# Diffusion block in f32 on one core: delta rule inverse in 32x32 blocks, attention heads in pairs, norm sums in few rows

## The reference

```
q, k = l2norm(q), l2norm(k)
# delta rule, in chunks: g is the cumulated gate
a   = strict_lower((k * beta) @ k.T * decay)
sol = triangular_solve(a + I, [v * beta, k * beta * exp(g)])
u, w = sol
v_new = u - w @ S
o     = (q * exp(g)) @ S + ((q @ k.T) * decay) @ v_new
S     = S * exp(g_last) + (k * exp(g_last - g)).T @ v_new
# both attentions
p = softmax(q @ k.T * scale [+ bias]);  o = p @ v
```

## Time and profile before

| what | us |
|---|---|
| median of 3 runs | 3280.55 (3277.18 to 3281.9) |
| the profiled execution | 3280.95 |
| its span in the trace | 3279.1 |
| TensorE busy | 2745.0 (84%), 13516 passes |
| VectorE busy | 1122.5 (34%) |
| ScalarE busy | 526.0 (16%) |
| GpSimd busy | 380.5 (12%) |

### The profile page before, as it was taken

The page is one execution under the profiler, slowest core; times in us unless marked ns, Lnnn a source line. Parts: engine busy times, 40 slices in busy tenths (PEclk is TensorE's granted clock), DMA queues, the critical chain, the costliest instruction groups (busy, mean ns, idle before and its releaser), DMA issues. The chain is left out here.

```text
span 3279.1 us, 34031 instructions
## 1 busy us (share of the span) xinstructions
PE 2745.0 (84%) x13516; PEld 1506.2 (46%) x13516; DVE 1122.5 (34%) x2055; ACT 526.0 (16%) x984; POOL 380.5 (12%) x380
## 2 busy tenths in 40 slices
PE   5899996778887679999999878999846685889896
PEld 3345563778776522222222236655736572222221
DVE  0143422454543512222222331740077733212123
ACT  1222116222221200000000010320222211000000
POOL 0000000444430000000000000000035400000000
PEclk9889997899998889999999879999968897999998
DMA  6300115100004268788887701101100134999996
GB/s 245 132 26 20 40 40 185 45 1 1 1 1 148 77 225 291 292 304 293 301 292 292 258 26 64 33 23 50 63 0 1 54 140 168 409 410 410 410 409 255
DMA packets 161760, 527.46 MB, mean 161 GB/s; under 512 B 13808, under 2 KB 49008, under 8 KB 155120
## 3 DMA queue, kind: packets, MB, share of 16 engines
q1 hardware_dynamic: 149920, 492.93, 40.1%
q10 hardware_dynamic: 7632, 18.27, 1.5%
q0 software_dynamic: 4096, 14.68, 1.4%
HBM read 516.93 MB, written 8.91 MB: 160 GB/s over the span
## 5 line engine op out<-in xcount | busy, mean ns | idle before, releaser
L1113 PE MATMUL bank<-arena 128*128 128x128 f32 x2208 | 271.2, 283 | 21.4 <-DVE arena L1285 19.7
L1113 PEld LDWEIGHTS bank<-arena 128*128 128x128 f32 x2208 | 263.6, 198 | 27.9 <-issue 24.5
L2037 PE MATMUL bank<-ring,arena 128*64 128x512 f32 x1024 | 258.9, 614 | 7.7 <-ACT arena L2092 7.2
L1993 PE MATMUL bank<-ring,arena 128*64 128x512 f32 x1024 | 245.6, 600 | 22.9 <-DMA ring<-in_moe_w_up_dram 22.8
L2128 DVE TENSOR_TENSOR arena<-arena,bank 128x512 f32<-128x512 f32 x160 | 109.9, 687 | 440.7 <-PE bank L1965 440.5
L1978 PE MATMUL bank<-ring,arena 128*64 128x512 f32 x1024 | 249.9, 609 | 10.6 <-DMA ring<-in_moe_w_gate_dram 9.4
L445 PE MATMUL bank<-arena,ring 128*128 128x384 f32 (+1 forms) x704 | 244.1, 509 | 2.7 <-ACTq L2288 1.5
L1965 PE MATMUL bank<-arena 128*128 128x512 f32 (+1 forms) x320 | 193.2, 687 | 44.8 <-DVE arena L2128 39.7
L445 PEld LDWEIGHTS bank<-arena,ring 128*128 128x128 f32 x704 | 134.4, 191 | 111.0 <-issue 33.0
L475 PE MATMUL bank<-ring,arena 128*128 128x256 f32 (+1 forms) x800 | 170.4, 375 | 6.9 <-ACTq L2288 6.9
L436 DVE COPY arena<-bank 128x384 f32<-128x384 f32 (+4 forms) x60 | 30.3, 505 | 423.2 <-PE bank L445 230.9
(11 more groups left out here) (304 smaller groups left out, 3411.3 us busy)
## 6 DMA issues: line engine op xcount, KB each, us to landing
ring<-in_moe_w_gate_dram SPq DMA_DIRECT2D x128, 1024.0 KB, 6.7
ring<-in_moe_w_up_dram SPq DMA_DIRECT2D x128, 1024.0 KB, 7.9
ring<-in_moe_w_down_dram SPq DMA_DIRECT2D x128, 1024.0 KB, 8.3
ring<-in_w_mod_dram SPq DMA_DIRECT2D x48, 1024.0 KB, 5.1
ring<-in_odd_w_in_dram SPq DMA_DIRECT2D x16, 1024.0 KB, 5.5
ring<-in_even_w_in_dram SPq DMA_DIRECT2D x10, 1024.0 KB, 10.3
ring<-in_even_w_out_dram SPq DMA_DIRECT2D x4, 1024.0 KB, 11.5
tok_lat_dram<-X ACTq DMA_DIRECT2D x8, 512.0 KB, 2.7
```

The costliest lines, as they stand in the source:

```text
L1113: mm = nc.tensor.matmul(heads(out[:, :])[:, h, :], lhs(h), rhs(h), start=start, stop=stop)
L1993: mm = nc.tensor.matmul(U_[half(hf), :], xl[:, k, :], columns(u, kk, hf), start=k == 0, stop=k == KB - 1)
L2037: mm = nc.tensor.matmul(D_[half(hf), :], HT[:, f % 4, half(f // 4)], columns(c, kk, hf), start=f == 0, stop=f == KB - 1)
```

## The change

It does five things.

- Delta scan: the inverse is built in 32x32 blocks. The four diagonal blocks of the four heads lie side by side in one 128x128 tile (`ATC`, `TTC`, `TC`, `WC`). Level 0 is a mask and a subtraction on VectorE, and a 32x32 block transpose there instead of the one on TensorE. Levels 1 to 4 multiply blocks only: 16 block products, a copy by ScalarE, 16 block products, a subtraction and a block transpose by VectorE. GpSimd spreads the blocks on the diagonal of the full inverse. Level 5 joins pairs of blocks, level 6 the two halves of 64, both writing into it. The two full products with the decay are made by VectorE between the levels. GpSimd makes the last right side (`KL`) at its end, with a wait of its own on TensorE.
- Both attentions: the unit is a pair of heads. 64-row products of the two heads alternate, in the neighbourhood attention their 64-column value products too. Score banks 0 to 3 belong to one pair at a time, turned tiles have banks 4 to 6, outputs bank 7. In the neighbourhood attention ScalarE scales the context scores (`plain`), and four bias tables are held instead of two.
- Norm: sums of four blocks go to four groups of 32 partitions, all eight into two banks; one logarithm and one exponential serve all; TensorE spreads the rows again, and VectorE multiplies out of PSUM in half blocks.
- Constants: 784 more columns (masks of 32x32 blocks, the block diagonal, selection rows and columns).
- The second scan uses twelve of the first scan's semaphores and adds 12 to each number it waits for. Its instructions stay.

The diff, cut to its core (removed code is left out for the most part, and so are changes that only rename):

```diff
...
+            parts[f"small{d}_{l}"] = np.concatenate([parts[f"level{d}_{l}"][b:b + 32, b:b + 32] for b in range(0, P, 32)])
+    parts["diag32"] = r // 32 == c // 32
...
+    parts["one_col"] = np.concatenate([np.broadcast_to(c[:, 0:32] == j, (P, 32)) for j in range(2)], 1)
+    parts["one_row"] = np.concatenate([np.broadcast_to(r % 32 == j, (P, P)) for j in range(2)], 1)
...
+                def front(p):
+                    parts, _ = segments(p)
+                    if p:
+                        nc.tensor.wait_ge(at_neg if biased(p) else at_exp, b + 2 * p)
+                    if pairs[p]["main"]:
+                        for e in range(2):
+                            for n, a, keys in parts:
+                                pairs[p]["main"](score(e, n)[:, 0:keys], e, n)
+                    for n, a, keys in parts:
+                        for e in range(2):
+                            mm = pairs[p]["tail"](score(e, n)[:, 0:keys], e, n)
+                            if n == len(parts) - 1:
+                                mm.then_inc(at_s, 1)
...
+                def values(p):
+                    tiles = segments(p)[1] // P
+                    nc.tensor.wait_ge(at_pt, bp + p + 1)
+                    if p:
+                        nc.tensor.wait_ge(at_oc, bp + p)
+                    if pairs[p]["together"]:
+                        for j in range(tiles):
+                            for e in range(2):
+                                mm = nc.tensor.matmul(out_rows(p, e), pairs[p]["v"](j, e), pt[:, tiles * e + j, :],
...
+                for p in range(np_ + 1):
+                    if p + 1 < np_:
+                        front(p + 1)
+                    if p:
+                        values(p - 1)
+                    if p < np_:
+                        turn(p)
...
+                for p in range(np_ + 1):
+                    if p < np_:
+                        if biased(p):
+                            plain(p)
+                        exps(p)
+                    if p:
+                        turned(p - 1)
...
+                            nc.vector.wait_ge(*loaded_)
+                            dv.then(nc.vector.scalar_tensor_tensor(r[:, 0:keys], score(e, n)[:, 0:keys], scale, bias,
+                                                                   ALU.mult, ALU.add))
+                            nc.vector.wait_ge(at_raw, i + 1)
+                            dv.then(nc.vector.tensor_reduce(m[:, 0:1], r[:, 0:total], AX.X, ALU.max))
...
+                mod.pe_rows(range(4))
+                for j in range(2):
+                    nc.tensor.wait_ge(nm_sq, 4 * j + 4)
+                    for bk, a, b_ in sums:
...
+                            mm = nc.tensor.matmul(bk[32 * g:32 * (g + 1), 0:b_ - a], one_col[:, j, :], SQ[g][:, a:b_],
+                                                  start=j == 0, stop=j == 1)
                     mm.then_inc(nm_sum, 1)
...
+                nc.tensor.wait_ge(nm_rs, 1)
+                for u, (i, hf) in enumerate(units):
+                    rows = slice(32 * (i % 4), 32 * (i % 4 + 1))
+                    if u >= len(spread):
+                        nc.tensor.wait_ge(nm_out, u - len(spread) + 1)
+                    nc.tensor.matmul(spread[u % len(spread)][:, 0:HALF], one_row[rows, i // 4, :], RS[rows, hf * HALF:(hf + 1) * HALF],
+                                     start=True, stop=True).then_inc(nm_bc, 1)
+                mod.pe_rows(range(4, KB))
...
+                    for l in range(1, 5):
+                        for d in range(2):
+                            nc.tensor.wait_ge(gd["bt"], step(n, l - 1, d, 4))
+                            nc.tensor.wait_ge(gd["tc"], step(n, l - 1, d, NS))
+                            for h in range(H):
+                                for i in range(NB):
+                                    mm = nc.tensor.matmul(compact(d, 2)[blk(i), h, :], BT[d][l][blk(i), h, :], TC[d][blk(i), h, :],
+                                                          start=True, stop=True)
+                            mm.then_inc(gd["u"], 1)
+                        for d in range(2):
+                            nc.tensor.wait_ge(gd["ucopy"], step(n, l - 1, d, NW))
+                            for h in range(H):
+                                for i in range(NB):
+                                    mm = nc.tensor.matmul(compact(d, 0)[blk(i), h, :], WC[d][blk(i), h, :], TTC[d][blk(i), h, :],
+                                                          start=True, stop=True)
+                            mm.then_inc(gd["upd"], 1)
...
+                            for s_, t_ in pairs32(d):
+                                mm = nc.tensor.matmul(compact(d, 2)[blk(t_), h, :], AT[d][blk(s_), h, blk(t_)], TC[d][blk(s_), h, :],
+                                                      start=True, stop=True)
...
+                            mm = nc.tensor.matmul(half64(d, 2)[far, h, :], AT[d][near, h, far], T64[d][near, h, :], start=True, stop=True)
+                        mm.then_inc(gd["u"], 1)
...
+                            mm = nc.tensor.matmul(half64(d, 0)[near, h, :], W64[d][far, h, :], TT[d][far, h, far], start=True, stop=True)
+                        mm.then_inc(gd["upd"], 1)
...
+                            nc.scalar.activation(WC[d], compact(d, 2), ACT.Copy).then_inc(gd["ucopy"], 1)
...
+                            nc.gpsimd.tensor_tensor(BT[d][l], ATC[d], small_mask(d, l), ALU.mult).then_inc(gd["bt"], 1)
+                    for d in range(2):
+                        nc.gpsimd.wait_ge(gd["tc"], step(n, 4, d, NS))
+                        nc.gpsimd.tensor_tensor(in_blocks(TT[d], NB), over_blocks(TTC[d], NB), diagonal(slice(0, P), range(NB)),
+                                                ALU.mult).then_inc(gd["asm"], 1)
...
+                        nc.gpsimd.wait_ge(gd["qkd"], 2 * n + d + 1)
...
+                        nc.gpsimd.wait_ge(gd["u"], step(n, 5, d, NW))
+                        nc.gpsimd.tensor_tensor(KL[d], heads(KTOK[:, tl, :]), gcol(EL, d, tl), ALU.mult).then_inc(gd["kl"], 1)
...
+                        for i in range(NB):
+                            nc.vector.tensor_tensor(ATC[d][blk(i), :, :], heads(bk(d, 3)[:, :])[blk(i), :, blk(i)], ETM[d][blk(i), :, blk(i)],
+                                                    ALU.mult).then_inc(gd["atc"], 1)
+                        nc.vector.wait_ge(gd["atc"], NB * (g + 1))
+                        dv.then(nc.vector.tensor_tensor(TTC[d], ATC[d], small_mask(d, 0), ALU.mult))
+                        dv.then(nc.vector.tensor_tensor(TTC[d], ident32, TTC[d], ALU.subtract))
+                        nc.vector.transpose(TC[d].rearrange("p h c -> p (h c)"), TTC[d].rearrange("p h c -> p (h c)")).then_inc(gd["tc"], 1)
+                    for l in range(1, 5):
+                        for d in range(2):
+                            nc.vector.wait_ge(gd["upd"], step(n, l - 1, d, NW))
+                            dv.then(nc.vector.tensor_tensor(TTC[d], TTC[d], compact(d, 0), ALU.subtract))
+                            nc.vector.transpose(TC[d].rearrange("p h c -> p (h c)"),
+                                                TTC[d].rearrange("p h c -> p (h c)")).then_inc(gd["tc"], 1)
+                            if l == 4:
+                                near = halves64(d)[0]
+                                nc.vector.wait_ge(gd["tc"], step(n, 4, d, NS))
+                                dv(nc.vector.tensor_tensor(in_blocks(T64[d][near, :, :], 2), over_blocks(TC[d][near, :, :], 2),
+                                                           diagonal(near, range(2 * d, 2 * d + 2)), ALU.mult))
+                        if l < 3:
+                            attention_of(n, l - 1)
+                        else:
+                            queries_of(n, l - 3)
...
+                        nc.vector.tensor_scalar(T64[d][blk(t_), :, SB * (s_ - 2 * d):SB * (s_ - 2 * d + 1)], compact(d, 2)[blk(t_), :, :], -1.0, None,
+                                                ALU.mult).then_inc(gd["t5"], 1)
+                        for s_, t_ in pairs32(d):
+                            nc.vector.tensor_scalar(TT[d][blk(s_), :, blk(t_)], compact(d, 0)[blk(s_), :, :], -1.0, None,
+                                                    ALU.mult).then_inc(gd["t5"], 1)
+                    for d in range(2):
+                        near, far = halves64(d)
+                        nc.vector.wait_ge(gd["upd"], step(n, 5, d, NW))
+                        nc.vector.tensor_scalar(TT[d][near, :, far], half64(d, 0)[near, :, :], -1.0, None, ALU.mult).then_inc(gd["tfin"], 1)
...
+        HG_STEP = dict(sig="in", cr="kbt", qk="diff", att="exps", att_used="pair", fin="qe", qfin="attn", turn="qkd", turncopy="rhs",
+                       out="kl", done="sol", zero="ws")
+        hg, HG_0 = {x: gd[y] for x, y in HG_STEP.items()}, 2 * NT
...
+                                    nc.tensor.wait_ge(hg["sig"], HG_0 + 2 * n + d + 1)
...
```

554 lines of the change are left out of this document (288 added, 266 removed).

## The result

The changed kernel takes 3109.5 us (median of 4 runs, 3101.4 to 3112.4) against 3280.3 of before on the same chip: ratio 0.948, 95% interval 0.946 to 0.950. That is 170.8 us less, where 152 were forecast, and the time lies in the forecast's own range. The profiled execution has a span of 3110.5 us.

A forecast was written before the change was run, and what follows sets the result against it. It took waits between engines to bound the scan, ScalarE to be nearly always busy in the norm, TensorE to bound both attentions. Gains of 105 + 18 + 10 + 20 - 1 = 152 us gave 3129, own range 3085 to 3175.

The forecast's parts named there:

- Levels 1 to 4: Scan step: block levels of 3.0 us each, 12 us for four, with 0.8 us per group of 32 passes.
- The way in: Scan step before the levels: seven instructions, 2.1 us per direction, 4.2 for both; 2.25 us gained a step.
- Levels 5 and 6: Scan step: joining blocks into the full inverse, 3.5 us for level 5 and 4.1 for level 6.
- The low clock: Scan step: small blocks leave the array mostly idle, the clock ends low, and the solution products lose 2.0 us.
- the 0.8 for GpSimd: Scan step: GpSimd's block diagonals and four products finish after levels 5 and 6, delaying the solution: 0.8 us lost.
- The second rival: Scan inverse: instruction supply holds TensorE at 0.112 us a pass, total 3431 us; chance 0.12, of which 0.10 slower.
- break-even of 0.072: Scan inverse: from 0.072 us a pass on, the changed kernel turns slower than before.
- The first rival: Scan block products: four row groups write one PSUM bank and go in file, 1.25 us a group, total 3179; chance 0.17.
- The half blocks: Norm: VectorE multiplies 16 half blocks of 384 columns out of PSUM, 0.56 us each, 9.0 us together.
- the wait behind the scores, 4.8: Latent attention, per pair: two maxima, one exponential and hand-overs take 4.8 us after 4.3 us of scores.
- The third rival: Both attentions: pairing heads gains nothing, as the single-buffered chain needs 1.4 us more per pair; total 3159, chance 0.11.
- the sign that the prediction set, under 70%: Neighbourhood attention: pairs 6.8 us apart with TensorE under 70% busy would show the forecast.

The follow-up runs named there:

- e5: Changed kernel with half the block products in levels 1 to 4, each twice as wide, the second head's inverse left out: 3092.6 us.
- e2: Changed kernel with the block product loops of levels 1 to 4 swapped, four heads of one diagonal block in a row: 3125.1 us.
- e6: Changed kernel with 32 more recorded TensorE passes of 128x128, results unread, before the levels of each scan step: 3116.3 us.
- e4: Changed kernel with the scaled copy of the context scores in the neighbourhood attention back on VectorE instead of ScalarE: 3122.5 us.
- e7: Changed kernel with the scan of before, the second scan having its own semaphores counted from zero: 3209.2 us.
- e9: The changed kernel itself measured again, with no edit: 3109.1 us.
- e8: Changed kernel with neighbourhood attention scores made head by head and the next pair's bias added between the two normalisations: 3110.9 us.
- e3: Changed kernel with GpSimd's scaling of the decayed queries moved behind its masks of the levels: 3100.1 us.

## Why the prediction was right, point by point

| term | forecast us | measured us |
|---|---|---|
| scan | 105 | 95.5 |
| norm | 18 | 19.7 |
| latent attention | 10 | 16.5 |
| neighbourhood attention | 20 | 40.3 |
| constants, and all else | -1 | -3.4 |
| sum | 152 | 168.6 (spans) |

Scan, norm and latent attention lie within the bounds that the prediction gave them. The neighbourhood attention does not: its 40.3 us are twice the forecast and outside 5 to 32.

**Scan.** From the first attention product to the end of the last update a step took 44.1 us (731.45 to 775.56) and takes 25.7 (615.99 to 641.26 + 0.43): 18.4 gained, on the mean of six steps 18.2, and 20.35 forecast. The way in was sized a little short: each direction takes 2.4 and not 2.1, the subtraction from the identity 0.43 and the four narrow products 1.24, so the second direction's blocks start 4.9 us behind the first product and not 4.2. Levels 1 to 4 take 13.0 us (620.91 to 633.93) and not 12. Three errors make this one. Four times 3.0 took level 1 whole from the second direction's first blocks on, where 1.9 us of it were left: 1.1 too much. The chain was too long by 0.5 in each of the other three levels (e5: 2.53 against 3.0), 1.4 together; 0.3 of each 0.5 are the two groups at 0.65 instead of 0.8. And the refill was missing, 3.5 us in three levels (11.1 against 7.6 in e5). That 12 came near 13.0 is luck, and a reader who only checked the sum of the levels would have passed all three. Levels 5 and 6 took 7.8 us (forecast 7.6). GpSimd cost nothing: its right sides were ready at 640.88, the inverse at 640.95. The low clock was right:

```profile
641.00:645.00 4.00, 4.00 (x21) 3.88 (x20) 0.43 (x1) 0.03 (x1) 1.87 (x2) 0.50 0.00 0
```

```profile
644.97 0.60 ACT L1342 ACTIVATE arena<-bank 128x512 f32<-128x512 f32 x1 [4.91 <-PE bank L1226]
...
646.89 0.60 ACT L1342 ACTIVATE arena<-bank 128x512 f32<-128x512 f32 x1 [0.84 <-PE bank L1226]
```

The first direction's solution products, from 641.15, took 3.7 us at 0.50, the second's 1.9. From the last update to the next step's first attention product 22.5 to 22.9 us pass against 20.4 to 21.3, on the mean 2.0 lost, where 2.8 were forecast: the 2.0 for the clock came, the 0.8 for GpSimd did not. A step so gained 16.3 us on the mean, six 98, of which 2 were lost around the steps. Of the reason that the prediction gave for the clock, the small blocks, e2 shows that they hold it at 0.50; what lowers it there, they or the waits between them, stays open (e6). "Six steps of 65.2" was the phase divided by six; a step of before is 64.5, which changed no term.

**The second rival was right in kind.** The supply of instructions does limit short passes, not at 0.112 us each but in portions: 128 passes in about 3.8 us, 0.030 a pass, under the break-even of 0.072 and under the 62 ns quoted beside this rival. It took 18.3 us of the scan ("issue" of L1256, L1271 and L1281: 16.8, 1.1 and 0.4) and did not decide. The trace of before could not have shown it: its fastest 128 passes in a row take 16.0 us (from 637.2 on). And that the supply is not held at 0.11 a pass stood in the earlier trace rows: sixteen passes in 1.05 us are 0.066, already under 0.072, though so short a series could have been queued. **The first rival** fell by the group of 0.65.

**Norm.** The steps held: the scaling factors were ready 15.5 us into the phase (16 forecast). The half blocks took less:

```profile
505.36 7.52 DVE L1001 TENSOR_TENSOR arena<-arena,bank 128x384 f32<-128x384 f32 x16 [9.10 <-PE bank L968]
```

VectorE's 16 (the row above) took 7.52 us, 0.47 each and not 0.56: 1.5 of the 1.7 us.

**Latent attention.** Mis-sized was the wait behind the scores, 4.8. From one pair's first score product to the next:

```profile
228.73 0.70 PE L812 MATMUL bank<-arena 128*128 128x512 f32 x1 [1.68 <-ACT arena L718]
...
237.15 1.13 PE L812 MATMUL bank<-arena 128*128 128x512 f32 x2
```

8.42 us, 4.34 of scores (to 233.07) and 4.08 for two maxima and the last exponential: the second head's maxima run beside the first one's exponentials, which the estimate counted apart. 0.8 us a pair in eight pairs is nearly all of the 6.5; the forecast's own items add to 11.8, and it rounded them to 10. The third rival (a pair needs 1.4 more) was wrong in both attentions.

**Neighbourhood attention.** The mechanism was right: TensorE went from 66 of 70 us busy (2050 to 2120 in before) to 54 of 70 (1930 to 2000), and VectorE and ScalarE alternate; e4 shows that their chain is the bound. Its 78% still miss the sign that the prediction set, under 70%. The size was not right. The rows of e4 give the chain: 4.06 us from the first biased score to the second exponential's start, 1.79 for that exponential, its reciprocal and normalisation, 5.85 together against 6.8. The estimate had 0.6 for the scaled copy, of which only 0.38 are waited for, and hand-overs of 0.4 that its other items already held. Sixteen pairs: 15 us. The other 5 were taken off for the start: four bias tables queue in front, but the first exponential came 8.3 us into the phase (1910.98) where it came after 9.9 (2043.41), so they cost nothing.

**Constants and all else.** The start lost 2.2 us (first projections at 55.4 instead of 53.2), which was made up before the latent attention. The expert loop took 2.4 us more, with no changed instruction. The stretch that holds it, from the gated norm to the neighbourhood attention, takes 1050.3 us in before and 1045.8 to 1051.9 in the traces of the changed code, so these 2.4 are not told from the spread. The second scan took 2.2 more. Its added 12 did not cost them (e7 has the same without it); where they come from stays open.

## What to carry to other kernels

Cutting one product into small blocks pays by the array's pace only as long as the instructions keep up. Here a portion was 128 passes of f32 and came each 3.8 us on the mean; no standstill was left where 128 passes lasted 4.06 us (e2) or 5.1 (e5, two levels of 2.53). Below that fewer and wider passes gain, as e5 shows, and a slower order costs less than its pace says (e2: 48.5 us of work, 13.6 of time). Where two engines alternate, add up the chain from end to end with each wait once; the overlap of the pair's halves is what an estimate by items misses.

## What the runs showed of the hardware

- Passes of 32 rows, 32 columns and 32 moving columns: 32 in 0.65 us and 64 in 1.27 at a granted clock of 0.50 when the block of the array changes between products, 32 in 0.45 us at 0.98 (e6), and 0.032 us each when eight in a row use one block (e2).
- TensorE stands still for 0.2 to 1.4 us after 128 such passes, 21 times in the scan of the changed kernel. The scan phase of the same code took 305.0, 304.8, 302.3 and 299.4 us with 18.3, 18.3, 17.1 and 15.2 us of such standstills (changed kernel, e9, e8, e4).
- The granted clock stands at 0.50 through 12 us in which TensorE is busy without a pause, with small blocks (e2); full products that follow the blocks from 641.15 on run at 0.50 until 645 and at 0.99 from then to 650.
- A product of 128x512 on VectorE takes 0.69 us alone and 1.76 beside one of GpSimd (e3).
- The 32x32 transpose of 128x128 on VectorE takes 0.31 us.
